# Expert rows turned by one VectorE instruction per tile instead of eight TensorE transposes, and the merge's first inputs loaded during the delta

## The reference, cut to what matters

```
q = (xb @ w_q).reshape(blk, PEER_HEADS, 2, PEER_D_HALF)
s = jnp.einsum('nhpd,phkd->nhpk', q, sub_keys)
sv, si = lax.top_k(s, PEER_TOPK)
...
tv, ti = lax.top_k(cand, PEER_TOPK)
eidx = jnp.take_along_axis(cidx, ti, axis=-1)
gates = jax.nn.softmax(tv, axis=-1)
u = jnp.take(u_tab, eidx, axis=0)
act = jax.nn.gelu(jnp.einsum('nd,nhkd->nhk', xb, u), approximate=False)
coef = gates * act
y = jnp.einsum('nhk,nhkd->nd', coef, jnp.take(v_tab, eidx, axis=0))
```

## Time and profile before

| | |
|---|---|
| median of 3 runs | 5883.69 us (5872.48, 5883.69, 5885.71) |
| the profiled execution's own time | 5870.38 us |
| its span (first to last instruction) | 5868.7 us |
| granted TensorE clock, mean | 0.982 of full |
| busy: PE, PEld (weight loads) | 5674.1, 5550.5 us (97%, 95%) |
| busy: DVE, ACT, POOL | 3186.5, 1321.3, 781.0 us (54%, 23%, 13%) |
| DMA moved | 584.42 MB, mean 100 GB/s |

### The profile page before, as it was taken

The page is one execution under the profiler, slowest core; times in us unless marked ns, Lnnn a source line. Parts: engine busy times, 40 slices in busy tenths (PEclk is TensorE's granted clock), DMA queues, the critical chain, the costliest instruction groups (busy, mean ns, idle before and its releaser), DMA issues. The chain is left out here.

```text
span 5868.7 us, 96409 instructions
## 1 busy us (share of the span) xinstructions
PE 5674.1 (97%) x36870; PEld 5550.5 (95%) x36870; DVE 3186.5 (54%) x7626; ACT 1321.3 (23%) x2393; POOL 781.0 (13%) x494
## 2 busy tenths in 40 slices
PE   8999999998998998998999999999999999999999
PEld 6999999986887997998999999999999999999998
DVE  3236401124764444899767665565555565555555
ACT  3113201122332112222333332111111121111112
POOL 0333323312221342232000000000000000000000
PEclk9999999999998998999999999999999999999999
DMA  4222224351113443111343335333333333333332
GB/s 156 61 66 94 98 83 128 96 173 48 47 45 112 133 133 104 58 58 51 129 157 150 144 145 170 87 91 98 94 87 87 87 91 93 99 87 87 87 87 81
DMA packets 706446, 584.42 MB, mean 100 GB/s; under 512 B 384808, under 2 KB 628520, under 8 KB 703333
## 3 DMA queue, kind: packets, MB, share of 16 engines
q1 hardware_dynamic: 650368, 419.21, 24.3%
q10 hardware_dynamic: 54784, 159.01, 7.8%
q0 software_dynamic: 1152, 4.19, 0.2%
HBM read 410.77 MB, written 171.59 MB: 99 GB/s over the span
## 5 line engine op out<-in xcount | busy, mean ns | idle before, releaser
L3358 DVE TENSOR_TENSOR yT<-yT,ex_y 128x352 f32<-128x352 f32 x1512 | 787.8, 521 | 907.6 <-PE ex_y L3213 907.6
L2557 PE MATMUL ea_banks<-h_high,ea_uT_high 128*128 128x352 f32 x3072 | 1011.1, 329 | 0.1
L2557 PE MATMUL ea_banks<-h_high,ea_uT_low 128*128 128x352 f32 x3072 | 987.4, 321 | 0.0
L2557 PE MATMUL ea_banks<-h_low,ea_uT_high 128*128 128x352 f32 x3072 | 987.0, 321 | 0.0
L3213 PE MATMUL ex_y<-ex_c_high,w_mb_high 128*128 128x352 f32 x3024 | 976.0, 323 | 4.5 <-DVE yT L3358 4.5
L3213 PE MATMUL ex_y<-ex_c_low,w_mb_high 128*128 128x352 f32 x3024 | 973.0, 322 | 0.0
L3213 PE MATMUL ex_y<-ex_c_high,w_mb_low 128*128 128x352 f32 x3024 | 971.8, 321 | 0.0
L2557 PEld LDWEIGHTS ea_banks<-h_low,ea_uT_high 128*128 128x128 f32 x3072 | 580.2, 189 | 0.0
L2557 PEld LDWEIGHTS ea_banks<-h_high,ea_uT_high 128*128 128x128 f32 x3072 | 579.0, 188 | 0.3 <-issue 0.3
L2557 PEld LDWEIGHTS ea_banks<-h_high,ea_uT_low 128*128 128x128 f32 x3072 | 577.3, 188 | 0.0
L3213 PEld LDWEIGHTS ex_y<-ex_c_high,w_mb_high 128*128 128x128 f32 x3024 | 568.4, 188 | 4.8 <-DVE yT L3358 4.8
(11 more groups left out here) (496 smaller groups left out, 9500.3 us busy)
## 6 DMA issues: line engine op xcount, KB each, us to landing
ex_gate<-tmp_gates SPq DMA_DIRECT2D x128, 528.0 KB, 6.0
w_mb_raw<-in_peer_v SPq DMA_DIRECT2D x128, 512.0 KB, 5.7
ea_u_raw<-in_peer_u ACTq DMA_DIRECT2D x126, 512.0 KB, 3.5
w_in_raw<-in_w_in SPq DMA_DIRECT2D x88, 512.0 KB, 3.7
tmp_acts<-ea_coef ACTq DMA_DIRECT2D x64, 528.0 KB, 2.7
tmp_gates<-yT SPq DMA_DIRECT2D x11, 3072.0 KB, 9.0
tmp_gates<-sg_out SPq DMA_DIRECT2D x11, 3072.0 KB, 9.0
ex_kept<-tmp_acts SPq DMA_DIRECT2D x64, 528.0 KB, 6.9
```

The costliest lines, as they stand in the source:

```text
L2557: last = pe.matmul(acts.banks[:, n, 0:CH], a[:, c, :], b[:, c, chunk(n)], start=(c == 0 and a is acts.uT_high[s] and b is high), stop=(c = ...
L3358: dve.tensor_tensor(at, at, ps_y[:, n, 0:CH], ALU.add).then_inc(summed, 1)
```

## The change

There are two parts.

First, the turn. A tile of `peer_u` is now loaded by four DMAs of 32 partitions, in runs of 32 floats (128 bytes), so that each 32x32 block lies in the partitions that its transpose belongs to. One VectorE `transpose` over 128x1024 then turns all blocks in place and writes `ps_t` with a stride of four. `turn_u` leaves the TensorE programs altogether and stands on VectorE right behind the `cut_u` of the tile before, in all three stages. The semaphore `u_in` counts four DMAs per tile.

Second, the merge. `yT` is allocated ahead of the delta, and `delta_prompt` now issues the two first weight loads and the eight loads of `ya` ahead of its loop and cuts the two weight tiles at the end of its GpSimd program. `merge_branches` does neither, and works in `yT` as `raw`, with a buffer of its own for `x2T`.

```diff
 def load_u(eng, acts, io, e, s):
-    eng.dma_start(acts.u_raw[:, s, :], io["peer_u"][ds(e * P, P), :]).then_inc(acts.u_in[s], 16)
-def turn_u(pe, k, acts, half, s, first=False):
+    rows = io["peer_u"][ds(e * P, P), :].rearrange("(r i) (k j c) -> j r (i k) c", i=SUB, j=SUB, c=BLOCK)
+    for j in range(SUB):
+        eng.dma_start(acts.u_raw[j * BLOCK:(j + 1) * BLOCK, s, :].rearrange("r (b c) -> r b c", c=BLOCK), rows[j]).then_inc(acts.u_in[s], 16)
+def turn_u(dve, acts, half, s, first=False):
     e = 2 * half + s
-    pe.wait_ge(acts.u_in[s], 16 * half + 16)
+    dve.wait_ge(acts.u_in[s], 16 * SUB * half + 16 * SUB)
     if not first:
-        pe.wait_ge(acts.uT_low_made, e)
-    for c in range(KT):
-        last = pe.transpose(acts.ps_t[:, c // 4, c % 4, :], acts.u_raw[:, s, c * P:(c + 1) * P], k["ident"][:, :])
-    last.then_inc(acts.u_turned, 1)
+        dve.wait_ge(acts.uT_low_made, e)
+    turned = acts.ps_t[:, :, :, :].rearrange("p b c n -> p (b c) n").rearrange("p k (r i) -> p i k r", i=SUB)
+    dve.transpose(turned, acts.u_raw[:, s, :].rearrange("p (i k c) -> p i k c", i=SUB, k=KT)).then_inc(acts.u_turned, 1)
...
@@ delta_prompt, SyncE: ahead of the loop; GpSimd: at the end
+            for u in range(2):
+                load_weights(sp, wt, io[BRANCHES[0][1]], u * P, u, u, first=True)
+            for kk in range(KT):
+                sp.dma_start(first[:, kk, :], tmp[BRANCHES[0][0]][:, kk, :]).then_inc(first_in[kk], 16)
...
+            for u in range(2):
+                cut_weights(pool, wt, u, 0, u, first=True)
...
@@ top_experts, VectorE, head(h)
                 search(h, 0, own, first)
                 cut_u(dve, acts, 2 * h + 2, 0)
+                turn_u(dve, acts, h + 1, 1)
                 search(h, 1, own, first)
                 cut_u(dve, acts, 2 * h + 3, 1)
+                turn_u(dve, acts, h + 2, 0)
...
@@ spread_gates, VectorE and TensorE
                         cut_u(dve, acts, 2 * half + s + 1, 1 - s)
+                        turn_u(dve, acts, half + 1, s)
...
-                        if n == 0:
-                            turn_u(pe, k, acts, half + s, 1 - s)
...
@@ experts, VectorE, turn(g)
                 cut_u(dve, acts, STASHED + 2 * g + 1, 1)
+                if not last:
+                    turn_u(dve, acts, STASHED // 2 + g + 1, 0)
```

More of the change, by code:

```diff
@@ L1541, in _, with delta_prompt @@
             half(1)
-def delta_prompt(nc, k, io, tmp):
+BRANCHES = (("ya", "w_br_conv"), ("yb", "w_br_gdn"), ("ym", "w_br_mem"))
+def delta_prompt(nc, k, io, tmp, first, first_in, wt):
     chunks = TP // P
@@ L2162, in multiply_by_rows, with merge_branches @@
             last.then_inc(row_done, 1)
-def merge_branches(nc, k, io, tmp, x2T, high, low, wt, wt_next, gain):
-    stages = (("ya", "w_br_conv"), ("yb", "w_br_gdn"), ("ym", "w_br_mem"))
+def merge_branches(nc, k, io, tmp, raw, first_in, high, low, wt, wt_next, gain):
+    stages = BRANCHES
     W0 = 3 * KT
@@ L2505 @@
 PAIRS = WIDE + (TOPK - TOP_A) * TOP_B
+BLOCK = 32
+SUB = P // BLOCK
 class Acts:
@@ L2819, in _ @@
         def _(dve):
+            turn_u(dve, acts, 0, 0, first=True)
             cut_u(dve, acts, 0, 0)
+            turn_u(dve, acts, 0, 1)
             for w in range(tiles):
@@ L3245, in last_values, with turn @@
                         turn_out(earlier)
-            def turn(g, last=False):
-                half = STASHED // 2 + g
-                turn_u(pe, k, acts, half, 1)
+            def turn(g):
                 products(g, 0)
                 values(LIVE, 2 * g - 1, 4 * g)
-                if not last:
-                    turn_u(pe, k, acts, half + 1, 0)
                 products(g, 1)
                 values(STASH, 2 * g, 4 * g + 2)
-            half = STASHED // 2
-            turn_u(pe, k, acts, half, 1)
             products(0, 0)
-            turn_u(pe, k, acts, half + 1, 0)
             products(0, 1)
@@ L3264, in _ @@
                 turn(g)
-            turn(pairs - 1, last=True)
+            turn(pairs - 1)
             last_values()
@@ L3490, in build @@
                 attend(nc, k, io, tmp, kT, v_rows, q, qs, q_in, qs_in)
[L3491 to L3494, removed]
         with nc.cleanup_on_exit(), nc.sbuf_tensor("yT", [P, KT, N], F32) as yT:
[L3496 to L3501, removed]
-                    merge_branches(nc, k, io, tmp, yT, high, low, wt_merge, wt_keys, gain(FFN))
-                    acts = Acts(nc, streams)
+            with ExitStack() as streams:
+                wt_merge = Weights(nc, streams, "w_mb")
+                wt_keys = Weights(nc, streams, "w_tk", slots_of=wt_merge)
+                first_in = [nc.alloc_semaphore(f"ya_in{kk}") for kk in range(KT)]
+                with nc.cleanup_on_exit(), ExitStack() as part:
+                    for name, shape in (("decays", [P, 3, NT, H]), ("beta_decay", [P, NT, H])):
+                        k[name] = part.enter_context(nc.sbuf_tensor(name, shape, F32))
+                    delta_prompt(nc, k, io, tmp, yT, first_in, wt_merge)
+                with nc.cleanup_on_exit(), ExitStack() as part:
+                    high = part.enter_context(nc.sbuf_tensor("h2_high", [P, KT, N], F32R))
+                    low = part.enter_context(nc.sbuf_tensor("h2_low", [P, KT, N], F32R))
+                    merge_branches(nc, k, io, tmp, yT, first_in, high, low, wt_merge, wt_keys, gain(FFN))
+                    acts = Acts(nc, part)
                     with nc.sbuf_tensor("picks", [P, 2 * NT * TOPK * TOPK], F32) as picks:
```

21 lines of the change are left out of this document (10 added, 11 removed).

## The result

The changed kernel takes 5904.8 us (median of 6 runs, 5900.0 to 5914.6), the kernel before 5878.3 (6 runs, 5865.7 to 5885.7): ratio 1.0048, 95% interval 1.0033 to 1.0063. It is slower by some 27 us, where 5855 was forecast.

What follows compares the result with a forecast made beforehand. TensorE was taken to bound the gates' and experts' stages, VectorE routing. Experts' -54, gates' +42, routing +5 and merge -8 make -15 us on the profiled 5870.4: 5855 us, range 5775 to 5905.

Steps and rivals of the forecast that it cites:

- budget: Gates' stage: time ScalarE's four load issues may take before its cast makes TensorE's sixth unit late, 2.8 us.
- term 2: Gates' stage: four issues on ScalarE ahead of its cast lose 77 us, transposes off TensorE gain 35: +42 us.
- two holds: Gates' stage: four issues hold ScalarE 2.8 us in one tile, 6.3 in the other, under the 3 MB store.
- Term 1: Experts' stage: transposes leave TensorE, gaining 0.88 us in each of 61 tiles, 54 us.
- the experiments' rival D: From the experiments, not the prediction: many short runs delay other transfers; no chance given.
- Term 3: Routing: start gains 7.3 us, VectorE pays 12.7 for 11 turns, tiles behind the heads nothing: +5 us.
- Term 4: Merge: slabs and weights loaded during the delta let it start 8 us sooner; from below, no gain.
- rival B: VectorE's transpose takes longer than 1.15 us; gain gone from 1.4 us on, 5922 us at 2.3; chance 0.15.
- A: Gates' stage: the issues don't hold ScalarE, so the full -35 is gained, 5778 us; chance 0.2.
- C: Gates' stage: issues hold longer, 3.7 and 7.2 us, making all tiles late, 40 us more, 5895; chance 0.12.
- D: Gates' stage: the store disturbs the loads half as much, 38 us less, 5817 us; chance 0.08.
- my own case: Whole kernel: the prediction's main account, 5855 us, with 5835 to 5880; chance 0.45.

Runs made afterwards that it cites:

- run 9: Changed kernel, issues still ahead of the cast, but each of a tile's four DMAs loads 32 whole rows: 5820.6 us, ratio 0.9899.
- run 7: Changed kernel plus 14 filler matmuls on TensorE in every second tile of the gates' stage, ahead of the waiting unit: 5881.8 us, ratio 1.0016.
- run 1: Changed kernel with the four issues of the next load moved behind the two casts in `raise_u`: 5791.6 us, ratio 0.9856.
- run 10: Changed kernel with one DMA per tile of 4096 runs of 128 bytes instead of four DMAs: 5785.0 us, ratio 0.9838.
- run 2: Changed kernel with one DMA of 128 whole rows per tile, VectorE's turn kept: 5785.8 us, ratio 0.9843.
- run 3: Kernel before with the block loads alone (four DMAs of 1024 runs per tile), TensorE still turning: 5932.3 us, ratio 1.0091.
- run 8: As run 1, but ScalarE instead of SyncE issues the first two tiles of expert rows in routing: 5788.6 us, ratio 0.9851.
- run 5: As run 1, but tiles 0 to 20 (routing) are loaded as whole rows and turned by TensorE: 5776.7 us, ratio 0.9831.

## Why the prediction was wrong

**The place was right, the budget and the clock were not.** I forecast a kernel 15 us faster, and it is slower. The step that failed is term 2, the gates' stage: +42 us forecast, +73 measured. It was named as the one that decides, and its two holds, 2.8 and 6.3 us, came out at 2.9 and 6.1 (means over the stage). But:

The *budget* of 2.8 us was too large. Three cases without a fall of the clock give it (a tile's length is the mean from one store issue of L2592 to the next, 3400.94, 3418.20 and 3440.38 in the rows above): a hold of 4.0 us makes a tile of 18.54 (run 9), 3.0 one of 17.41 and 6.1 one of 20.61 (run 7), where 16.87 is the tile without a hold in the way (run 1). Tile = 16.9 + hold - 2.4 each time, to 0.1 us. The missing 0.4: from start to start the cut and the turn take 2.49 us and not my 2.36 (3426.91 to 3429.40); two small gaps, from the cast to the cut and from the last key to the matmul, make 0.14; and behind each of its two waits TensorE's block of eight takes 1.16 us instead of 1.06. I had also read only one kind of tile: in the undisturbed one the issues start 0.85 us behind the first copy (3401.42 to 3402.27) and not 0.53. So the undisturbed tiles lose about 0.5 us each where I had none, and 22 x (0.5 + 3.7) = 92 us are lost where I had 77; measured 832.4 - 740.8 = 91.6.

The *clock* was missing from the sum. I priced the late keys at their lateness alone. The 18 falls make it 852.3 instead of 832.4: 20 us. (Where I write of 19 in the expectation of run 1, the first is the low stretch at the stage's start, which the kernel before has too.) This step failed outright. The profile before could not show a fall in this stage, but the earlier trace rows showed an engine at full clock that I was about to let idle for 2.5 us at a time.

Against that the *transposes* gave more: 779.3 - 740.8 = 38.5 us instead of 35, so the slower first matmul went too. Gates' stage in all: -38.5 + 91.6 + 19.9 = +73, forecast +42.

**The mechanism of the hold was wrong, though its sizes fitted.** I let the fourth issue wait until enough runs were through. In fact an undisturbed issue of 1024 runs takes about 0.6 us, four with gaps 2.8 to 2.9, held by nobody; that the sum agreed is chance. Under the store it is the second and third issue that are held: 0.60, 1.59 and 2.83 us, then a short fourth. Runs 9 and 10 show that both things count: four DMAs of 32 runs are held 4.0 us, four of 1024 6.1, and one of 4096 not at all. What the queue counts stays open.

The DMA rate of those loads was near my reading: about 216 GB/s where the 16 DMA engines are full with them (within 3402 to 3408), so 9.5 ns per run of 128 bytes and engine. The Trainium skill's rule of three cycles per packet ("DMA: Bandwidth & Descriptors", "Why small descriptors are slow") gave the estimate 10.4; the trace is 9% under it.

**Term 1, experts' stage**: forecast -54, measured -51.9, by the mechanism named; ScalarE's issues take 2.8 to 3.5 us for four there and nobody waits. But its start takes 5.9 us more, which I left at nothing. Whole rows bring it back (38.1 in run 2), another order of issue and cast doesn't (44.2 in run 1), so it goes with the short runs. The DMA engines are full there (share 1.02 in the row above), and beside 8192 short runs the second gate load lands 25.7 us after the stage's last one-hot matmul instead of 21.8, and the first `v` tile after 26.9 instead of 23.6; TensorE then waits 5.0 us for ScalarE (4.6 in run 1, 1.5 in run 2, none before), and its clock is 0.84 against 0.91. Here the experiments' rival D is right, but its size is not explained: in run 3 the same short runs, with TensorE's turn, make a start of 40.2, one load of 4096 runs makes 42.2 (run 10), and the kernel before itself takes 38.0 and 39.3 in its two profiles.

**Term 3, routing**: forecast +5, measured +12.1. The middle was right: from the second search to the last `picks` reduction it takes 12.5 us longer, against 12.7. The start was not: the second search gains 2.4 us instead of 7.3. The query product does go at once, and the first key is transposed 4.2 us sooner, but the last key only 1.5; run 8 excludes SyncE's order as the cause. The loads and the clock may have a part in it: in runs 9 and 10, with four loads of whole rows and one load of 4096 runs per tile, the first search starts 59.4 and 59.9 us behind the first issue instead of 62.3, and TensorE, which runs at half clock while it waits for keys, is back at full speed some 4 us sooner. But run 2, with whole rows in one load, has 61.6, so the cause stays open. The tail took 2.0 us, where I had nothing and 1.4 as the other end. The granted clock is lower in this stage too (0.93 against 0.96), but run 1, with 1.7 us less of lost clock from the second search to the last reduction, took the same 419.0 us for it, so the clock is hardly what lengthens it. Run 5 takes 11 us of all this back.

**Term 4, merge**: forecast -8, measured 5.4 at the first matmul, 5.8 behind the stage.

**The turn**: forecast 1.15, measured 1.260 us. An estimate by the Trainium skill ("Vector Engine (DVE) Microarchitecture Reference", section 3.8) was 1.07; the trace lies above both, and as rival B priced it this is 6 us. From its start to the next instruction's it is 1.17 us, and the cut ahead of it takes 1.32 instead of 1.21. That is in the parts above. Of the prediction's rivals A, C and D did not happen, and B's condition, 1.4 us, was not met. That the result still lies just inside the range, at its upper end, is luck: no case of mine had its cause. With the clock's 20 us and the budget's 15 my own case would have been slower.

From the forecast: -15 + 31 (gates) + 6 (start) + 7 (routing) + 2 (merge) + 2 (experts) = +33.

## What to carry to other kernels

What stands ahead of an instruction in its own engine's order costs that engine's time, DMA issues too. Put the instruction that another engine waits for first and the prefetch behind it: here one moved line turns +0.5% into -1.4%. Where a full engine will have to idle, price the fall of its clock as well as the wait. Move work only out of the stage where its engine is the bound: in routing the same turn costs 11 us, and run 5 leaves it on TensorE there, at -1.7%.

## What the runs showed of the hardware that I had not expected

- An issue's time hardly depends on its runs: 0.32 us for 32 rows, 0.35 for 128, 0.57 for 1024 runs into 32 partitions, 0.39 for 4096 over 128 partitions. In the gates' stage the second and third of four loads issued in a row were held under a 3 MB store of another engine, and a load issued alone never was.
- A VectorE transpose of 128x1024 fp32 out of SBUF into PSUM takes 1.260 us, the same to 3 ns in 128 cases.
- After idling some 2.5 us, or 2.5 and 0.65, TensorE ran some 3.4 us at 1.2 GHz (6.9 once), in 18 of 21 such places. After 0.2 to 0.7 and 0.65 us it did not, in the profiled execution of run 3. 308 matmuls that compute nothing of use, 14 ahead of every such place, made the stage 19.9 us shorter.
